# Two feed-forward seven-product pairs relaid around a plain unit, with two of their four weight sums made by adding transfers

## The reference, cut to what matters

```python
def swiglu_ffn(x, w_in, w_out):              # w_in: 1024 x 5632, w_out: 2816 x 1024
    gate, up = jnp.split(x @ w_in, 2, axis=-1)
    return (jax.nn.silu(gate) * up) @ w_out

for i in range(DEPTH):                        # DEPTH = 2
    x = x + 0.5 * swiglu_ffn(rms_norm(x, ffn1_norm[i]), ffn1_w_in[i], ffn1_w_out[i])
    xn = rms_norm(x, mix_norm[i])
    ...                                       # i = 0: pooling and convolution; i = 1: spatial gating
    x = x + y
    x = x + 0.5 * swiglu_ffn(rms_norm(x, ffn2_norm[i]), ffn2_w_in[i], ffn2_w_out[i])
return rms_norm(x, final_norm)
```

## Time and profile before

| what | value |
|---|---|
| median of three runs | 1018.74 us |
| the profiled execution | 1020.88 us |
| its span, first to last instruction | 1019.1 us |
| PE busy | 892.8 us, 88% |
| DVE busy | 730.5 us, 72% |
| ACT busy | 491.4 us, 48% |
| POOL busy | 80.5 us, 8% |
| transfers | 181.92 MB, mean 179 GB/s |
| granted TensorE clock, mean | 0.94 of full speed |

### The profile page before, as it was taken

The page is one execution under the profiler, slowest core; times in us unless marked ns, Lnnn a source line. Parts: engine busy times, 40 slices in busy tenths (PEclk is TensorE's granted clock), DMA queues, the critical chain, the costliest instruction groups (busy, mean ns, idle before and its releaser), DMA issues.

```text
span 1019.1 us, 10498 instructions
## 1 busy us (share of the span) xinstructions
PE 892.8 (88%) x4006; PEld 737.5 (72%) x4006; DVE 730.5 (72%) x734; ACT 491.4 (48%) x535; POOL 80.5 (8%) x70
## 2 busy tenths in 40 slices
PE   9399989679998599899695998997799969988986
PEld 8278778568886478688584786885589857877865
DVE  6779779356966887786558797764588677967934
ACT  7346446236954455454353464542474444644522
POOL 0000000046920000000020000000200000000000
PEclk9799989979999699899997999998899989998998
DMA  9936733564356648432867375526775573673332
GB/s 290 299 103 202 241 103 128 172 220 138 132 165 194 199 145 262 140 135 94 257 203 262 98 237 161 186 94 211 219 257 180 169 258 103 212 229 120 114 138 73
DMA packets 152826, 181.92 MB, mean 179 GB/s; under 512 B 8205, under 2 KB 137257, under 8 KB 152776
## 3 DMA queue, kind: packets, MB, share of 16 engines
q1 hardware_dynamic: 152184, 180.72, 54.5%
q10 hardware_dynamic: 592, 0.53, 0.2%
HBM read 168.11 MB, written 1.05 MB: 166 GB/s over the span
## 4 chain that ended last, share of the span: by engine, by line
PE 52%; DVE 22%; DMA 10%; SPq 9%; ACT 4%; issue 3%; POOL 0%; POOLq 0%; ACTq 0%; DVEq 0%
DVE w_lo L1096 12%; PE acc L1615 6%; PE acc L1616 5%; PE acc L1617 5%; DMA xs<-xs 5%; SPq L390 5%; PE ga L1615 4%; PE ga L1616 4%; PE ga L1617 4%; PE tp L1617 4%; PE tp L1616 4%; PE tp L1615 4%; PE ub L1615 3%; PE ub L1617 3%; PE ub L1616 3%; DMA raw<-in_ffn_w_out_dram 3%
## 5 line engine op out<-in xcount | busy, mean ns | idle before, releaser
L705 ACT ACTIVATE w_hi<-raw 128x2048 fp32r<-128x2048 f32 x119 | 227.0, 1912 | 156.8 <-DMA raw<-in_ffn_w_out_dram 91.1
L1096 DVE TENSOR_TENSOR w_lo<-raw,w_hi 128x2048 fp32r<-128x2048 f32 x111 | 252.5, 2283 | 65.7 <-ACT w_hi L705 65.6
L1615 PE MATMUL acc<-w_hi,act_hi 128*128 128x512 f32 x416 | 170.0, 409 | 33.4 <-DVE act_lo L1295 33.4
L1615 PE MATMUL ga<-w_hi,xn_hi 128*128 128x512 f32 x256 | 109.6, 428 | 74.4 <-DVE sgh L1281 52.6
L1616 PE MATMUL acc<-w_lo,act_hi 128*128 128x512 f32 x416 | 166.5, 400 | 0.0
L1617 PE MATMUL acc<-w_hi,act_lo 128*128 128x512 f32 x416 | 166.1, 399 | 0.0
L1096 DVE TENSOR_TENSOR w_lo<-scratch,w_hi 128x2048 fp32r<-128x2048 f32 x48 | 109.6, 2284 | 17.5 <-ACT w_hi L705 17.5
L1615 PEld LDWEIGHTS acc<-w_hi,act_hi 128*128 128x128 f32 x416 | 81.4, 196 | 53.1 <-DVE w_lo L1096 21.9
L1615 PEld LDWEIGHTS ga<-w_hi,xn_hi 128*128 128x128 f32 x256 | 52.1, 203 | 90.2 <-DVE w_lo L1096 79.1
L705 ACT ACTIVATE w_hi<-scratch 128x2048 fp32r<-128x2048 f32 x48 | 91.7, 1911 | 35.6 <-PE acc L1617 27.4
L1616 PE MATMUL ga<-w_lo,xn_hi 128*128 128x512 f32 x256 | 106.3, 415 | 0.0
(11 more groups left out here) (213 smaller groups left out, 1356.1 us busy)
## 6 DMA issues: line engine op xcount, KB each, us to landing
raw<-in_ffn_w_in_dram SPq DMA_DIRECT2D x108, 512.0 KB, 6.0
raw<-in_ffn_w_out_dram SPq DMA_DIRECT2D x88, 512.0 KB, 4.4
scratch<-in_ffn_w_in_dram SPq DMA_DIRECT2D x48, 512.0 KB, 8.2
xs<-xs SPq DMA_DIRECT2D x176, 64.0 KB, 2.1
gain<-in_ffn_w_in_dram SPq DMA_DIRECT2D x16, 512.0 KB, 7.6
raw<-in_sgu_w_in_dram SPq DMA_DIRECT2D x16, 512.0 KB, 7.2
raw<-in_ab_w_in_dram SPq DMA_DIRECT2D x12, 512.0 KB, 5.3
raw<-in_ab_w_out_dram SPq DMA_DIRECT2D x8, 512.0 KB, 3.7
```

The costliest lines, as they stand in the source:

```text
L705: act.activation(w_hi[:, slot_of[n], :], slab(n), ACT.Copy).then_inc(hi_split, 1)
L1096: dve.tensor_tensor(w_lo[:, slot_of[n], :], slab(n), w_hi[:, slot_of[n], :].bitcast(F32), ALU.subtract).then_inc(lo_split, 1)
L1615: pe.matmul(dst, s_hi, m_hi, start=start, stop=False, skip_group_check=onto)
```

## The change

The pairs now start at slabs b+6 and b+21, and a plain unit stands inside each pair, between the products B11 and B21 (`between`): unit 3 in pair one, unit 7 in pair two. The three w_out slabs 0 to 2 (4 to 6) follow T1 in a row, the fourth stands before T4. T1 goes into the bank `ga` (`row[0]`) instead of `tp`.

The sums are now T1 = Q0 - Q2 (DVE), T3 = Q3 - Q2 and T2 = T1 + Q3, T4 = Q1 - T2 (DVE). ACT turns the sign of Q2 in place (`negate`), and POOL issues two transfers that add Q3 to what stands in the quads of Q2 and Q0 (`add_blocks`); the second waits until T1 has been split. The sign of T1's token sum is turned to fit.

On ACT and DVE the gates and products of a plain unit stand ahead of `hidden_hi` and `hidden_lo` of the unit before, and half by half between splits. On SP the first blocks are turned earlier among the loads, w_out slabs 8 and 9 are loaded ahead of the blocks of unit 8 (`to_turn(d + 9)`), and the last blocks are turned between the next stage's second and third slab. The transposes of `taps` and `columns` go behind mixer 0's first unit, and POOL's `windows` behind the norm of mixer 0, with only the fills left in the first FFN.

```diff
-    SEVEN = (8, 23)
+    SEVEN = (6, 21)
-    B11, B21, T1, T2, B22, T3, T4 = 0, 1, 3, 5, 6, 7, 9
+    B11, B21, T1, T2, B22, T3, T4 = 0, 3, 4, 8, 9, 10, 12
-    SUM_OF = {T1: 1, T2: 2, T3: 3, T4: 4}
+    SUM_OF, ADDED = {T1: 1, T4: 2}, {T2: 0, T3: 1}
-    OUT_AT = [z + at for z in SEVEN for at in (2, 4, 8, 10)] + [36, 37, 38]
+    OUT_AT = [z + at for z in SEVEN for at in (5, 6, 7, 11)] + [36, 37, 38]
...
+            def add_blocks(p, n):
+                pool.wait_ge(negated, p + 1)
+                pool.wait_ge(quad_landed[3], 32 * (p + 1))
+                pool.dma_start(quads[2], quads[3], accum_op=ALU.add).then_inc(added_up[ADDED[T3]], 16)
+                pool.wait_ge(lo_split, n + T1 + 1)
+                pool.dma_start(quads[0], quads[3], accum_op=ALU.add).then_inc(added_up[ADDED[T2]], 16)
...
+            def negate(p):
+                act.wait_ge(sum_ready, 2 * p + SUM_OF[T1])
+                act.activation(quads[2], quads[2], ACT.Copy, scale=-1.0).then_inc(negated, 1)
...
-                    split_to(b + 6)
+                    split_to(b + 4)
+                    gate_of(0, 1, 1, 2)
+                    split(b + 5)
                     side_hi_of(k, 0, 0)
                     side_hi_of(k, 1, 1)
+                    gate_of(1, 1, 1, 2)
                     hidden_hi(k, 0)
+                    split(b + 6)
                     split(b + 7)
-                    gates(1, 1, 2)
+                    gate_of(0, 2, 2, 4)
                     split(b + 8)
+                    gate_of(1, 2, 2, 4)
+                    negate(p)
                     hidden_hi(k, 1)
...
-                to, left, right = {T1: (0, 2, 0), T2: (0, 3, 0), T3: (2, 3, 2), T4: (1, 1, 0)}[what]
+                to, left, right = {T1: (0, 0, 2), T4: (1, 1, 0)}[what]
...
+                bank_w = row[0]
                 multiply(n + B11, bank_x, xn_hi[:, 0:4, first], xn_lo[:, 0:4, first], True)
+                between()
                 multiply(n + B21, bank_z, xn_hi[:, 4:8, first], xn_lo[:, 4:8, first], True)
+                pe.wait_ge(side_ready, 4 * stage + 1)
+                pe.wait_ge(ga_free, fill0[k] + v)
+                multiply(n + T1, bank_w, sums_hi[:, 0], sums_lo[:, 0], True)
                 outs(0)
-                pe.wait_ge(joined, 3 * p + 1)
+                outs(1)
+                outs(2)
                 pe.wait_ge(side_ready, 4 * stage + 4)
-                multiply(n + T1, bank_z, sums_hi[:, 0], sums_lo[:, 0], True)
-                outs(1)
...
                 multiply(n + T3, bank_x, sums_hi[:, 3], sums_lo[:, 3], False)
-                outs(2)
+                outs(3)
                 multiply(n + T4, bank_x, xn_hi[:, 4:8, other], xn_lo[:, 4:8, other], False)
-                outs(3)
...
+                    out_of(8, 36)
+                    out_of(9, 37)
                     to_turn(d + 9)
-                    out_of(8, 36)
+                    out_of(10, 38)
                     to_turn(d + 10)
-                    out_of(9, 37)
-                    out_of(10, 38)
+                    if k + 1 < len(stages):
+                        first_loads(k + 1, d + STEPS)
...
-                    if k + 1 < len(stages):
-                        first_loads(k + 1)
-                    to_turn(d + STEPS)
```

More of the change, by code:

```diff
@@ L279, in hybrid_trunk @@
         sum_ready = sem("sum_ready")
+        negated = sem("negated")
+        added_up = [sem(f"added_up{j}") for j in range(2)]
         side_step = sem("side_step")
@@ L439, in first_loads @@
                         load_rows(base[k] + j, sgu_w_in[0], j, pair(D, WIDTH))
+                if turned is not None:
+                    to_turn(turned)
                 if kind == "ffn":
@@ L929, in _ @@
-                    side_hi_of(k, 3, 1)
                     split(b + 9)
-                    gates(2, 2, 4)
                     split(b + 10)
+                    split(b + 11)
+                    gates(3, 3, 7)
                     hidden_hi(k, 2)
-                    split(b + 11)
-                    gates(3, 3, 6)
                     seven(k, SEVEN[0], 4)
+                    split(b + 21)
+                    split(b + 22)
+                    hidden_hi(k, 5)
+                    gate_of(0, 4, 6, 19)
@@ L937, in _ @@
+                    negate(p + 1)
+                    gate_of(1, 4, 6, 19)
                     split(b + 23)
-                    hidden_hi(k, 5)
                     split(b + 24)
-                    gates(4, 6, 19)
                     split(b + 25)
+                    gate_of(0, 5, 7, 22)
+                    split(b + 26)
+                    gate_of(1, 5, 7, 22)
                     hidden_hi(k, 6)
-                    split(b + 26)
-                    gates(5, 7, 21)
                     seven(k, SEVEN[1], 8)
+                    split(b + 36)
@@ L946, in _ @@
+                    split(b + 37)
+                    gate_of(0, 6, 10, 34)
                     hidden_hi(k, 9)
+                    gate_of(1, 6, 10, 34)
                     split(b + 38)
                     nxt = b + 39
-                    gate_rows(0, b + 34, r + 6, f + 10, ACT.Silu, scaled=late)
                     split_to(b + 39)
-                    gate_rows(1, b + 34, r + 6, f + 10, ACT.Silu, scaled=late)
+                    hidden_hi(k, 10)
                     split_to(b + 40)
-                    hidden_hi(k, 10)
@@ L1432, in _ @@
                     side_sums(True)
-                    hidden_lo(k, 0)
+                    half(1, 0)
+                    split(b + 5)
+                    half(1, 1)
+                    blocks_of(1)
                     side_lo(k, 0, 0)
                     side_lo(k, 1, 1)
+                    split(b + 6)
                     split(b + 7)
-                    unit(1)
+                    half(2, 0)
+                    weight_sum(p, T1)
+                    half(2, 1)
                     split(b + 8)
-                    weight_sum(p, T1)
@@ L1440, in _ @@
-                    side_sums(False)
-                    hidden_lo(k, 1)
-                    side_lo(k, 2, 0)
-                    side_lo(k, 3, 1)
+                    blocks_of(2)
                     split(b + 9)
-                    unit(2)
                     split(b + 10)
-                    hidden_lo(k, 2)
+                    half(3, 0)
                     split(b + 11)
-                    unit(3)
+                    half(3, 1)
+                    blocks_of(3)
                     seven(k, SEVEN[0], 4)
+                    split(b + 21)
@@ L1451, in _ @@
+                    split(b + 22)
+                    weight_sum(p + 1, T1)
+                    half(6, 0)
+                    half(6, 1)
                     split(b + 23)
-                    weight_sum(p + 1, T1)
-                    hidden_lo(k, 5)
+                    blocks_of(6)
                     split(b + 24)
-                    unit(6)
                     split(b + 25)
-                    hidden_lo(k, 6)
+                    half(7, 0)
                     split(b + 26)
-                    unit(7)
+                    half(7, 1)
@@ L1460, in _ @@
+                    blocks_of(7)
                     seven(k, SEVEN[1], 8)
+                    split(b + 36)
+                    split(b + 37)
+                    half(10, 0)
                     hidden_lo(k, 9)
+                    to_blocks(0, f + 10)
+                    half(10, 1)
+                    to_blocks(1, f + 10)
                     split(b + 38)
                     nxt = b + 39
-                    unit(10)
+                    split_to(b + 39)
                     if k == 0:
```

223 lines of the change are left out of this document (117 added, 106 removed).

## The result

The changed kernel takes 901.85 us (median of four runs, 899.16 to 903.53), the kernel before 1018.72 us beside it: ratio 0.8848, 95% interval 0.8822 to 0.8874. The profiled execution has a span of 897.4 us.

A forecast was written before the change was run, and what follows sets the result against it. PE's work and its waits were taken as the bound. 1019.1 - 118.9 (waits) - 24 (clock) + 4 x (1.5 + 2 + 2.5) + 2 (POOL) + 4 (clock) = 906.2 us span, median 906; range 883 to 958.

The forecast's parts named there:

- The forecast's own case: Whole kernel: median 906 us, own range 885 to 932 us; chance 0.67, counted together with DVE becoming the bound (925 us).
- A: Rival: the turned blocks stay late, so third waits and most of the tails stay; +45, 951 us; chance 0.18.
- B: Rival: an adding transfer takes 25 us and two overlap, making T2 late in the pairs; 965 us; chance 0.08.
- C: Rival: a pair's two adding transfers run one after the other and share engines with loads; about 1075 us; chance 0.07.
- First and second wait: PE's `ga` waits at units 1 and 2 of a stage, the first 15.48 us: both go with gates first.
- Third wait and tail: Unit 7's 4.21 us wait and the tail's 5.57 + 3.14 us: gone, with 2 and 2.5 us left.
- DVE's work: In the pairs: 27 or 28 us of 30 to 33, fits but close; 1.5 us a stage left for it.
- The adding transfers: POOL's two transfers a pair: 8 us each, no stall; DMA engines at 68 to 81%, hurting only at a stage's start.
- T2's slack: Room for T2's adding transfer before PE needs T2: 20 us in pair one, 17 us in pair two.
- The lower bound: Cost of one adding transfer from below: 3.65 us, a slab at the measured transfer rate.
- POOL and `tp`: The 11.2 us `tp` wait goes with its transposes; POOL's later windows delay low parts and pair sums, 2 us.
- The clock: PE's lower clock after long waits: 2.0 us for three waits in each of four FFNs, 24 us; 4 us remain.

The follow-up runs named there:

- e3: Kernel before with gates and products of units 1 and 2 ahead of the turned blocks' parts, half by half, on ACT and DVE: 1005.09 us, ratio 0.9838.
- e2: Changed kernel with the gates of units 1, 2, 3 and 7 behind the turned block again, on ACT alone: 906.85 us, ratio 0.8885 to kernel before.
- e5: Changed kernel with units 0 and 1 turned late again, behind the loads, on SP alone: 921.76 us, ratio 0.9003 to kernel before.
- e7: Kernel before with unit 0 turned right behind Q0 and unit 1 right behind Q2 on SP: 1027.86 us, ratio 1.0055.
- e11: Changed kernel with the tail of SP's list as before: 935.12 us, ratio 0.9152 to kernel before.
- e1: Changed kernel with all four weight sums on DVE, no sign change or adding transfers: 885.46 us, ratio 0.8675 to kernel before.
- e9: Changed kernel with only T3 by adding transfer and T2's sum on DVE: 881.74 us, ratio 0.8619 to kernel before.
- e10: Changed kernel with only T2 by adding transfer, T3's sum on DVE, no sign change: 883.41 us, ratio 0.8642 to kernel before.
- e12: Changed kernel with only T3 by transfer and both mixers' gains loaded ahead of the next stage's first slabs: 876.01 us, ratio 0.8574 to kernel before.

## Why the prediction was right, point by point

*The forecast* was 906 us for the median, and 906.2 for the span; they were 901.85 and 897.4. The forecast's own case held; A, B, C did not. That the total came so near is in part luck: terms that were 17 us too high and 12.6 us too low largely cancel.

*First and second wait.* Gone, as worked out. In the changed kernel's third stage unit 2 starts at 291.4 and B21 at 315.93, 24.5 us later, and the prediction had 352.0 - 327.5 = 24.5: PE never stands still on this stretch. But "the first wait goes" was put down to the gates' place, with the loads only checked for being in time. The gates' place alone was worth 16 us in the old layout (e3) and some 4 in the new one (e2); SP's early turning (e5: 0.0155, 16 us) and the split of b+6 moved behind the gate are as much a part of it. And in the chain ahead of the gate the prediction named b+6 and the turned block but not DVE's side sums between them. ACT waited 4.52 us for the first of these, in the kernel before as in e7, and 1.62 us for the block:

```profile
334.06 0.63 ACT L839 ACTIVATE w_hi<-xs 128x512 fp32r<-128x512 f32 x1 [4.52 <-DVEq L1313]
```

*Third wait and tail.* I left 2 and 2.5 us a stage, 18 us in all; 1.0 us is left. The step that held the tail just covered was too careful, since nothing in it was late. e11 puts a price on the tail's order, 0.030 of 1019, 31 us, with the clock in it, near the 33.4 us of the earlier trace rows.

*DVE's work.* 27 to 28 us of 30 were forecast to the end of T1. The window:

```profile
291.40:321.40 30.00, 30.00 (x134) 24.82 (x134) 27.65 (x27) 17.10 (x17) 1.78 (x2) 1.00 0.99 275
```

27.65 of 30.00. DVE's total is 699.1 us against 695. But I read this as close to a bound, and took the term of 1.5 us a stage for it. e1 puts two more sums on DVE in each pair, 736.9 us in all, and is faster. The wait of 3.2 us a stage at w_out slab 1 came from the step next to it, the adding transfers.

*The adding transfers.* As a dependency the step was right: 9.7 us from issue to landing (median; 8.4 to 12.8 over all 16) against the 8 taken and the bounds of 3.65 and 25, far within T2's slack of 17 to 20 us. As a load it was half right. 9.3% of 897.4 us is 83 us of the 16 engines, 5.2 us for each transfer (against 58 to 174), and the share of the two queues is 71% (68 to 81%). The lower bound mixed two measures: 3.65 us is the time in which 1 MiB arrived with the engines at 0.90, while the engines' own time for it is 61.6% of 897.4 us for 180.72 MB, 3.2 us. What failed is the sentence "It hurts only at a stage's start, where the share is 0.90 already". The two transfers fill a stretch of their own, 0.99 for 25 us around T1, just when w_out slab 1 is fetched, and the one for T2 lands ahead of that load. The Trainium skill (DMA: Bandwidth & Descriptors, "Issuing engines are not separate DMA queues") has the engines shared by all issuers; the trace agrees: the 512 KB loads of w_out land after 4.6 us in e1, and after 6.1 with POOL's transfers beside them. The term was 1.5 and should have been 3.2 us a stage; with the rest of both transfers together cost 0.8848 - 0.8675 = 0.017 of the old time, 17.6 us.

*POOL and `tp`.* The `tp` wait is gone. Two us were forecast for mixer 0 behind POOL, and none came: the wait of 1.2 us for POOL's `avg` is at the program's start, as before. What I missed is the wait at mixer 1's norm, 5.3 us; no term of the sum has it. Its gain load is late, and 2.1 us of it is the product that ran beside POOL.

*The clock.* Matmuls that start 0.43 us apart in place of 0.23 number 128 before and 32 after, and 15 before and 4 after, nearly all of them the first behind a wait, have the next one 0.56 to 0.60 us behind them. That makes 31 and 8 us of loss, against 24 and 4 in the sum.

*Where the 8.8 us between 906.2 and 897.4 lie.* Time without a matmul fell by 97.5 us (126.3 to 28.8) where the sum has 92.9, and PE's busy time by 24.2 (892.8 to 868.6) where it has 20. Of the 4.6 us in the first: third waits and tails 17 us less; w_out slab 1 6.7 us more (12.7 for 6); the norms 5.9 us more; POOL 2 us less. That makes 6.4 less, and waits under 1 us take the rest back. Of the 4.2 us in the busy time the clock accounts for 3 (31 - 8 = 23 in place of 20); the rest stays open.

## What to carry to other kernels

List everything that stands ahead of a late instruction on its engine, not only what ended its wait: here the data of a slab, a sum on DVE and a turned block stood in a row ahead of one gate. Taking one of them out of the row gave 1.6% or nothing, two gave 3.5%. Moving arithmetic from a busy engine to the DMA engines pays only where a load that is wanted soon doesn't end up beside or behind it: one transfer a pair was free, a second one cost 0.017 of the old time, and the engine it spared had had the room all along. The share of the DMA engines warns of it but doesn't decide it: 0.98 over 30 us went without a wait, 0.99 over 25 us did not. Look up, for each load that is wanted next, what is issued before it.

## What the runs showed of the hardware

An adding transfer of 1 MiB from SBUF to SBUF took 5.2 us of the 16 engines' time, where 1 MiB of weights took 3.2 in the same run, and 8.4 to 12.8 us to landing beside loads; POOL was occupied for 0.9 us to issue one. That is 1.6 times a plain load, and not three times, which was the bound that I took for reading two streams and writing one.

In a norm the gain's product on DVE, 128 x 512, takes 0.75 us. In e9 one of the 21 took 5.0, the second of these two. It began at 185.12, 0.61 us after a low part on POOL, and ended at 190.13, 0.55 us after it (DVE, then POOL):

```profile
184.45 5.68 DVE L1186 SCALAR_TENSOR_TENSOR xs<-xres,rstd,gain 128x512 f32<-128x512 f32 x2 [1.63 <-DMA gain<-in_mix_norm_dram]
```
```profile
184.51 5.07 POOL L626 TENSOR_TENSOR w_lo<-raw,w_hi 128x2048 fp32r<-128x2048 f32 x1 [1.05 <-ACT w_hi L724]
```

The first product, which began 0.06 us before POOL's, took 0.75. In e1 and e10 the second one also took 5.0 us and ended 0.55 us after POOL's low part, and the 2.88 us product at mixer 1 in the changed kernel began 2.15 us into one of 4.49 us and ended 0.55 us after it. So in e9 a DVE idle for 1.6 us at a late gain became a wait of 3.6 us for PE. In e12 the same product, with its gain there in time, runs at 186.60, ahead of POOL's low part at 187.62, and two of them take 1.41 us:

```profile
186.60 1.41 DVE L1190 SCALAR_TENSOR_TENSOR xs<-xres,rstd,gain 128x512 f32<-128x512 f32 x2 [0.68 <-POOL rstd L623]
```

That agrees with what the Trainium skill says (SBUF — State Buffer, "Who interferes with whom"): a DVE instruction with two inputs in SBUF contends with a GpSimd instruction that reads SBUF, the ports that they share are locked for one of the two, and the order of issue decides which one is held. No run moved POOL's part alone, so the cause itself is the page's and the coincidence in time is what was measured.
